# Modulation chunks in one spare place, a tenth chunk place, and split refills in a two-layer diffusion step with experts

## The chip, the cores and the metric

The kernel runs on one core of a Trainium2 chip, in one launch. The metric is device microseconds of that core, median of three runs; lower is better. The core's engines are TensorE (PE, with PEld for its weight loads), VectorE (DVE), ScalarE (ACT), GpSimd (POOL) and SyncE (SP), which here issues every DMA transfer, in program order, into one queue that 16 DMA engines share.

## The reference

Two trunk layers over 128 context tokens and 256 sample tokens, width 1024, float32. In each layer, for both token groups with the same weights:

```python
sh1, sc1, g1, sh2, sc2, g2 = silu(cond) @ w_ada + b_ada          # 6 x 1024
h = rms_norm(x, norm1_g) * (1 + sc1) + sh1
z = h @ w_in                       # four token mixers, then 4 x 1024 gate logits
branches = [conformer_conv, fourier_mix, window_attention, neighbourhood_attention]
proj = einsum("blnc,ncd->blnd", branches, w_branch)
x = x + g1 * ((sigmoid(gates) * proj).sum(n) @ w_out)
h = rms_norm(x, norm2_g) * (1 + sc2) + sh2
aff = softmax(h @ w_router)        # 16 experts, each picks its top 16 / 32 tokens
y = (silu(xs @ w_gate) * (xs @ w_up)) @ w_down * affinity
x = x + g2 * scatter_add(y)
```

At the end come one RMSNorm per group and the keys and values of the context tokens. Nearly all the traffic is weights: of 536.71 MB that the profile counts, 2 x 16 experts x 12.6 MB = 403 MB are expert weights.

## The kernel before

**Units and places.** Weights come in units of 2 MB, each one DMA transfer of 128 partitions x 4096 words: 12 modulation units a layer (ada0 to ada11), 12 of the input projection (w0 to w11), two of the branch projections (wb01, wb23) and two of the output projection (wo0, wo1). They go to a ring of seven places in SBUF (`ring`, slots 0 to 6). The list `order` is the order in which SyncE issues them, and a unit may be issued only when the unit before it in its place has been used (`used_up`). ada4, ada8 and ada9 have slot 6 (`SPARE`); ada5, ada6, ada7 and ada10 share slots 0 and 1 with the input projection, so that w4 stands behind ada5, w5 behind ada6 and w8 behind ada7. ada10 and ada11 are multiplied in the routing.

**The mixer.** TensorE, in one order written out by hand, makes 48 output tiles of the input projection (`zt`, L961; every weight is split into a high and a low part by ScalarE, L1245, and GpSimd, L893). The last 32 are the gate tiles, numbered idx 0 to 31, eight to each branch, and w4 to w11 serve four each. Between them stand attention, the branch products (L1157) and, at the numbers in `ADA_AT`, the modulation products (L701). ScalarE splits the weights of a tile two tiles ahead, in program order, so a late unit holds up all that ScalarE does after it.

**Output projection and routing.** Six tiles of products with `wo` (L1225) follow, with transposes (L1175) and router logits (L1184) between them; then a chain through VectorE and ScalarE makes the softmax and the top choice (L1685 to L1948).

**Experts.** Each expert is six chunks of 2 MB: 0 to 3 gate and up, two rows of 128 inputs (k) each, 4 and 5 down; a layer has 96, numbered x. They turn through nine places (`PLACE`): two in the arena (`LOW`, whose fourth part lies in `C` and which is thus two transfers, and `HIGH`) and the seven slots of the ring. `first_chunk` fetches 0 to 7 as their places come free, `experts_sync` the ninth and then, in order, each chunk when the chunk nine before it has been used (`used_chunk`). TensorE's products are L1800 (gate and up) and L1829 (down). Four experts make a group; a group begins with a gather of its tokens (L1768) and ends with the combination (L1846). At a layer's end SyncE issues ada0 to ada3 and w0 of the next.

Of the kernel before, what the change touches and what calls it, by code (L numbers as in the profile page):

```python
# [22 lines left out]
F32 = mybir.dt.float32  # L23
F32R = mybir.dt.float32r
ALU = mybir.AluOpType
# [115 lines left out]
def build(nc, A):  # L141
    ctx = ExitStack()
    with ctx:
# [78 lines left out]
        def adas(c):  # L222
# [36 lines left out]
        assert cursor[0] <= ARENA, cursor[0]  # L259

# [21 lines left out]
        BRL = over("BRL", "XN", 0, 8 * TOK)[:, :].rearrange("p (b c t) -> p b c t", b=4, c=2)  # L282
# [25 lines left out]
        AT = part(KT * 64).rearrange("p (k s) -> p k s", k=KT)  # L308
        assert cursor[0] <= pr_at, cursor[0]
# [10 lines left out]
                 "cum_ready sel_ready selg_ready e_pair e_down_half silu_done x_done prompt_part wo_high wo_rest mrg_high mrg_rest").split() + list(OPENING)  # L320
        land = [sem(f"land{s}") for s in range(NSLOT)]
        e_land = [sem(f"e_land{s}") for s in range(9)]
        full = [sem(f"full{b}") for b in range(8)]
        free = [sem(f"free{b}") for b in range(8)]
        e_full = [sem(f"e_full{b}") for b in range(8)]
# [3 lines left out]
            wo_high=8, wo_rest=8, mrg_high=8, mrg_rest=8, x_mixed=6, b_high=32, b_rest=32, br_high=4, br_rest=4, rest_in=16, grow_in=64, sink_in=16, cache_in=64, nab_in=16,  # L329
# [8 lines left out]
        def stood(layer, name):  # L338
# [6 lines left out]
        ADA_AT = {2: 4, 5: 5, 8: 6, 11: 7, 14: 8, 17: 9}  # L345
# [4 lines left out]
        order = ["ada0", "ada2", "ada1", "ada3", "w0", "w1", "w2", "w3", "w6", "wb01", "ada4", "w7", "ada5", "w4", "ada6",  # L350
                 "w5", "ada8", "ada7", "w8", "wb23", "ada9", "w9", "w10", "w11", "wo0", "wo1", "ada10", "ada11"]
# [5 lines left out]
        done_at.update({f"ada{c}": 23 + c for c in IN_ROUTING})  # L357
        FIXED = {"ada0": 4, "ada2": 5, "ada1": 1, "ada3": 2, "ada11": 5, "ada4": SPARE, "ada8": SPARE, "ada9": SPARE}
# [13 lines left out]
        MRGH = over("MRGH", "ring", 4 * 4 * D, KT * TOK)[:, :].rearrange("p (k t) -> p k t", k=KT)  # L372
        MRGL = over("MRGL", "arena", mrg_at, KT * TOK)[:, :].rearrange("p (k t) -> p k t", k=KT)
# [66 lines left out]
        for n in GATE_ORDER:  # L440
            for k in range(KT):
# [9 lines left out]
                if idx in ADA_AT:  # L451
                    tile_a(f"ada{ADA_AT[idx]}")
                if idx - 1 in ADA_AT:
                    ada_small_tiles(ADA_AT[idx - 1])
        for t in range(TT):
            for half in range(2):
                T.add(f"wo{t}_{half}", 2 * t + half)
# [1656 lines left out]
```

## Time and profile before

| | us |
|---|---|
| median of three runs (lowest, highest) | 1673.03 (1672.55, 1674.01) |
| the profiled execution, its own time | 1671.89 |
| its span | 1670.0 |
| TensorE products busy | 1557.3 (93%) |
| VectorE, ScalarE, GpSimd busy | 524.9, 490.0, 353.6 |
| DMA, mean over the span | 321 GB/s |

Stages overlap, and the shares are means over stages with different limits. What ends a stage is read from its own stretch: the busy share of the DMA engines there, and what TensorE waits for. In the timeline a row gives start, duration (of a merged row from the first start to the last end), engine and line, and in brackets how long the engine was idle just before, and for whom. A float32 product stands as two records.

### The profile page before, as it was taken

How to read it: one execution, taken by the hardware profiler on the slowest of the kernel's cores; microseconds unless marked ns; L12 is line 12 of the kernel's file. 1: busy time of each engine (PE TensorE's matmuls, PEld its weight loads, DVE VectorE, ACT ScalarE, POOL GpSimd, SP SyncE). 2: the span in 40 equal slices, each digit the busy share in tenths (PEclk: the TensorE clock that was granted, in tenths of full speed). 3: DMA queues.
4: the chain of work that ended last, by engine and by line, in shares of the span. 5: the costliest groups of instructions: out<-in, count | busy, mean ns of one | idle time of the engine just before them, and what ended most of it. 6: DMA issues, size and time to landing. Idle time of an engine off the chain costs nothing.

```text
span 1670.0 us, 20051 instructions
## 1 busy us (share of the span) xinstructions
PE 1557.3 (93%) x8363; PEld 956.0 (57%) x8363; DVE 524.9 (31%) x864; ACT 490.0 (29%) x908; POOL 353.6 (21%) x196
## 2 busy tenths in 40 slices
PE   7999999999999999799799999999999998988986
PEld 4998889984333343242269978899633433423322
DVE  3734454633121121121159244545411211212013
ACT  4444454433112020121153545434320211211212
POOL 1654355820000000000035634468000000000000
PEclk9999999999999999999999999999999999999999
DMA  9643452279999999999994425525799999999995
GB/s 380 243 156 110 199 202 101 105 318 425 428 426 426 426 427 427 428 427 427 422 388 168 156 102 202 202 77 232 327 423 426 426 427 428 427 427 427 427 427 233
DMA packets 52097, 536.71 MB, mean 321 GB/s; under 512 B 13584, under 2 KB 13992, under 8 KB 20008
## 3 DMA queue, kind: packets, MB, share of 16 engines
q1 hardware_dynamic: 52008, 535.43, 77.7%
q8 instruction: 67, 1.10, 0.3%
q14 instruction: 22, 0.18, 0.0%
HBM read 533.05 MB, written 2.36 MB: 321 GB/s over the span
## 4 chain that ended last, share of the span: by engine, by line
PE 68%; DMA 24%; DVE 3%; ACT 2%; issue 1%; POOL 1%; SPq 0%; DVEq 0%; ACTq 0%
PE psum L961 22%; PE psum L1800 16%; DMA ring<-in_w_e_down 14%; PE psum L1829 8%; DMA ring<-in_w_e_gu 8%; PE psum L1225 4%; PE psum L1157 3%; PE psum L1768 3%; PE psum L1846 2%; PE psum L701 2%; DMA ring<-in_w_ada 1%; DMA ring<-in_w_in 1%; PE psum L1125 1%; PE psum L695 1%; PE psum L1104 1%
## 5 line engine op out<-in xcount | busy, mean ns | idle before, releaser
L961 PE MATMUL psum<-HTH,WSR 128*128 128x384 f32 x1536 | 413.0, 341 | 8.4 <-ACT arena L1360 6.1
L1800 PE MATMUL psum<-ring,arena 128*64 128x512 f32 x1504 | 339.7, 596 | 28.1 <-DMA ring<-in_w_e_gu 26.7
L961 PEld LDWEIGHTS psum<-HTH,WSR 128*128 128x128 f32 x1536 | 280.3, 188 | 22.2 <-issue 11.6
L893 POOL TENSOR_TENSOR WSR<-ring,WSR 128x1024 fp32r<-128x1024 f32 x92 | 220.2, 2394 | 260.7 <-ACT WSR L1245 260.7
L961 PE MATMUL psum<-HTL,WSR 128*128 128x384 f32 x768 | 259.2, 337 | 0.0
L1800 PEld LDWEIGHTS psum<-ring,arena 128*64 128x64 f32 x1504 | 103.4, 137 | 233.0 <-issue 186.1
L1977 DVE TENSOR_TENSOR arena<-arena,psum 64x512 f32<-64x512 f32 x64 | 44.1, 690 | 503.6 <-PE psum L1800 315.5
L1829 PE MATMUL psum<-ring,arena 128*64 128x512 f32 x864 | 193.5, 596 | 5.2 <-DMA ring<-in_w_e_down 5.2
L1245 ACT ACTIVATE WSR<-ring 128x1024 fp32r<-128x1024 f32 x96 | 101.7, 1059 | 299.7 <-PE psum L961 289.2
L961 PEld LDWEIGHTS psum<-HTL,WSR 128*128 128x128 f32 x768 | 144.8, 189 | 0.1
L1883 ACT ACTIVATE arena<-psum 64x512 f32<-64x512 f32 x64 | 37.6, 588 | 348.5 <-PE psum L1800 348.3
L1800 PE MATMUL psum<-arena 128*64 128x512 f32 x456 | 124.0, 597 | 11.1 <-DMA C<-in_w_e_gu 7.5
L1829 PEld LDWEIGHTS psum<-ring,arena 128*64 128x64 f32 x864 | 61.1, 137 | 118.7 <-issue 117.2
L1888 ACT ACTIVATE arena<-psum 32x512 f32<-32x512 f32 x64 | 37.7, 589 | 269.7 <-PE psum L1829 269.3
L864 POOL MEMSET arena<- 128x888 f32 x2 | 2.1, 1039 | 513.0 <-PE psum L701 513.0
L1966 DVE TENSOR_TENSOR arena<-psum,GROW 32x512 f32<-32x512 f32 x64 | 43.8, 684 | 212.0 <-PE psum L1829 211.6
L624 ACT ACTIVATE arena<-psum,MOD,SC 128x128 f32<-128x128 f32 (+1 forms) x144 | 57.1, 460 | 136.1 <-PE psum L1768 130.8
L1800 PEld LDWEIGHTS psum<-arena 128*64 128x64 f32 x456 | 36.7, 136 | 82.8 <-issue 68.8
L1561 DVE TENSOR_TENSOR arena<-arena 128x384 f32<-128x384 f32 x48 | 78.6, 1638 | 1.7
L1768 PEld LDWEIGHTS psum<-arena,XN 128*128 128x128 f32 x384 | 47.0, 191 | 37.4 <-issue 37.4
L1494 DVE SCALAR_TENSOR_TENSOR psum<-arena,PRM,psum 128x414 f32<-128x414 f32 x116 | 64.7, 646 | 0.0
L1558 DVE TENSOR_TENSOR arena<-arena,psum 128x384 f32<-128x384 f32 x48 | 26.6, 554 | 113.9 <-ACT arena L1360 99.6
(221 smaller groups left out, 1730.7 us busy)
## 6 DMA issues: line engine op xcount, KB each, us to landing
ring<-in_w_e_gu SPq DMA_DIRECT2D x94, 2048.0 KB, 31.2
ring<-in_w_e_down SPq DMA_DIRECT2D x54, 2048.0 KB, 31.2
ring<-in_w_ada SPq DMA_DIRECT2D x24, 2048.0 KB, 13.1
ring<-in_w_in SPq DMA_DIRECT2D x22, 2048.0 KB, 8.0
arena<-in_w_e_gu SPq DMA_DIRECT2D x22, 1536.0 KB, 29.2
arena<-in_w_e_gu SPq DMA_DIRECT2D x12, 2048.0 KB, 29.8
arena<-in_w_e_down SPq DMA_DIRECT2D x10, 2048.0 KB, 31.5
C<-in_w_e_gu SPq DMA_DIRECT2D x22, 512.0 KB, 31.0
```

The costliest lines, as they stand in the source:

```text
L624: return nc.scalar.activation(dst, src, ACT.Identity, scale=SC[:, which, k, i:i + 1], bias=MOD[:, sec * KT + k, i:i + 1])
L893: nc.gpsimd.tensor_tensor(WSR[:, 1, i % 2], part_src(i), WSR[:, 0, i % 2].bitcast(F32), ALU.subtract).then_inc(S["w_rest"], 1)
L961: ins = nc.tensor.matmul(ps[:, 0:TOK], WSR[:, w, i % 2, k, :], x[:, k, :], start=(k == 0 and w == 0 and x is HTH), stop=(k == KT - 1 and w ...
L1157: ins = nc.tensor.matmul(ps[:, 0:TOK], w[:, idx % 2, c, :], x[:, c, :], start=(ins is None), stop=(c == 1 and w is BWL))
L1225: ins = nc.tensor.matmul(ps[:, :], x[:, k, t * P:(t + 1) * P], w[half][:, k, :], start=(k == 0 and turn == 0), stop=(k == KT - 1 and turn ...
L1245: nc.scalar.activation(WSR[:, 0, i % 2], part_src(i), ACT.Copy).then_inc(S["w_high"], 1)
L1494: ins = nc.vector.scalar_tensor_tensor(acc if k < CONV_K - 1 else ACC[:, c, :], U[:, c, k:k + AW], w, acc, ALU.mult, ALU.add)
L1561: nc.vector.tensor_tensor(MRG[:, k, :], MRG[:, k, :], GP[:, idx % 2, :], ALU.add).then_inc(S["gate_add"], 1)
L1768: ins = nc.tensor.matmul(ps[:, c0:c0 + P], XN[:, t, k * P:(k + 1) * P], SEL[:, AT_PLACE[t]].rearrange("p e s -> p (e s)"), start=(t != 2), ...
L1800: ins = nc.tensor.matmul(pb[half][64 * m:64 * m + 64, :], XE[:, k, j, :], w[:, half * CH:(half + 1) * CH], start=(k == 0), stop=(k == KT - 1))
L1829: ins = nc.tensor.matmul(ps[64 * half:64 * half + 64, :], AT[:, k, :], chunk_row(x, k % 4)[:, half * CH:(half + 1) * CH], start=(k == 0), ...
L1977: e_release(nc.vector.tensor_tensor(AA[0:64, cols], TMP[64:128, cols], ps[64:128, :], ALU.mult), f"gu{j}_{half}")
```

## The change

- ada4 to ada10 all go through the spare place (slot 6), one after the other. The order of the units is new: w4, w5 and w8 go ahead of ada5, ada6 and ada7, ada8 after ada7, ada10 before w10. ada10 is multiplied in the mixer, at idx 20.
- The merged branches' high part (`MRGH`) moves from slot 4 to `XN`, the low part of the last branch to slot 5, half of the squares to the arena and the transposed activations (`AT`) into `XE`. So slot 4 is free once the last attention output is copied, and takes chunk 0, which is issued after w11. Slot 0 takes chunk 1, after wo1.
- Chunk 8 goes once to a tenth place, half in `GROW[:, 0]` and half in `once_slot`, after the residual sum and the router's exponentials. It is never refilled; the others turn through nine places as before.
- Chunks 10, 11 and 12 come as two transfers each (the last of them, in `LOW`, as three instead of two), the first half when the first half of the place is used (`e_first`), the rest at the old wait. The last gate-up chunk comes as halves, the last down chunk as quarters, and the last expert takes both halves of the output row after row.
- Router: three idle products instead of one, after the last logits; the last transpose goes ahead of the logits of its tile. The combination waits for halves of the last expert's output, and the last output row goes out in two halves.

```diff
@@ units
-        ADA_AT = {2: 4, 5: 5, 8: 6, 11: 7, 14: 8, 17: 9}
+        ADA_AT = {2: 4, 5: 5, 8: 6, 11: 7, 14: 8, 17: 9, 20: 10}
...
-                 "w5", "ada8", "ada7", "w8", "wb23", "ada9", "w9", "w10", "w11", "wo0", "wo1", "ada10", "ada11"]
+                 "ada6", "w8", "ada7", "ada8", "wb23", "ada9", "w9", "ada10", "w10", "w11", "wo0", "wo1", "ada11"]
...
-        FIXED = {"ada0": 4, "ada2": 5, "ada1": 1, "ada3": 2, "ada11": 5, "ada4": SPARE, "ada8": SPARE, "ada9": SPARE}
+        FIXED = {"ada0": 4, "ada2": 5, "ada1": 1, "ada3": 2, "ada11": 5, **{f"ada{c}": SPARE for c in range(4, 11)}}
@@ places of the chunks
-            PLACE = (LOW, HIGH, unit_at["wo0"][0], SPARE, unit_at["wo1"][0], 3, 4, unit_at["ada10"][0], unit_at["ada11"][0])
+            third = 3 - unit_at["wo0"][0] - unit_at["wo1"][0]
+            PLACE = (4, third, LOW, HIGH, unit_at["wo0"][0], SPARE, unit_at["wo1"][0], 3, unit_at["ada11"][0])
...
+            ONCE = RING - 1
+
+            LAST_UP, LAST_DOWN = NE * PER - 3, NE * PER - 1
...
+                if x == ONCE:
+                    sp.dma_start(GROW[:, 0].rearrange("p i d -> p (i d)"), src[:, 0:2 * D]).then_inc(once_land, 16)
+                    sp.dma_start(once_slot, src[:, 2 * D:4 * D]).then_inc(once_land, 16)
+                    return
+                if x == LAST_DOWN:
+                    for r in range(4):
+                        sp.dma_start(chunk_row(x, r), src[:, r * D:(r + 1) * D]).then_inc(down_land[r], 16)
+                    return
...
@@ first_chunk, and when
+                    if s == 4:
+                        copied(sp, f"o{len(ATT) - 1}")
...
+                    elif name == "w11":
+                        first_chunk(0)
                     elif name == "wo1":
-                        first_chunk(0)
-                sp.wait_ge(S["out_kv"], base("out_kv") + 64)
-                for x in range(1, RING - 1):
+                        first_chunk(1)
+                        sp.wait_ge(S["out_kv"], base("out_kv") + 64)
+                        first_chunk(2)
+                for x in range(3, RING - 1):
                     first_chunk(x)
@@ experts_sync
+                sp.wait_ge(S["x_mixed"], base("x_mixed") + 2 * TT)
+                sp.wait_ge(S["router_exp"], base("router_exp") + 1)
+                fetch(sp, ONCE, chunk(l, ONCE // PER, ONCE % PER))
                 used_up(sp, "ada11")
...
-                for x in range(RING, NE * PER):
-                    used_place_of(x - RING)
-                    fetch(sp, x, chunk(l, x // PER, x % PER))
+                for x in range(RING + 1, NE * PER):
+                    before_it = turn(x) - RING + (turn(x) - RING >= ONCE)
+                    src = chunk(l, x // PER, x % PER)
+                    if before_it < PAIRS - 1:
+                        sp.wait_ge(S["e_first"], base("e_first") + before_it + 1)
+                        fetch_first_rows(sp, x, src)
+                        used_place_of(before_it)
+                        fetch_last_rows(sp, x, src)
+                    else:
+                        used_place_of(before_it)
+                        fetch(sp, x, src)
...
@@ router, TensorE
+                transposed(2, 1)
                 logits(2, 0)
-                transposed(2, 1)
-                idle_products(T.at["wo2_0"][0], 1)
                 logits(2, 1)
-                ada_main(pe, l, 10)
+                idle_products(T.at["wo2_1"][0], 3)
@@ experts_tensor, gate and up
+                            if g == 0 and j == 0 and k in (0, 2, 4):
+                                ins.then_inc(S["e_first"], 1)
```

On SyncE in the mixer of a layer, the seven transfers after the context keys and values have gone out, before: ada5, w4, ada6, w5, ada8, ada7, w8.

```order
L848 DMA ring<-in_w_ada 128x4096 [waits w_rest]
L848 DMA ring<-in_w_in 128x4096 [waits full0]
L848 DMA ring<-in_w_ada 128x4096 [waits w_rest]
L848 DMA ring<-in_w_in 128x4096 [waits full2]
L848 DMA ring<-in_w_ada 128x4096 [waits full2]
L848 DMA ring<-in_w_ada 128x4096 [waits w_rest]
L848 DMA ring<-in_w_in 128x4096 [waits full3]
```

The same seven in the list of after: w4, ada5, w5, ada6, w8, ada7, ada8.

```order
L908 DMA ring<-in_w_in 128x4096 [waits w_rest]
L908 DMA ring<-in_w_ada 128x4096 [waits full2]
L908 DMA ring<-in_w_in 128x4096 [waits w_rest]
L908 DMA ring<-in_w_ada 128x4096 [waits full0]
L908 DMA ring<-in_w_in 128x4096 [waits w_rest]
L908 DMA ring<-in_w_ada 128x4096 [waits full2]
L908 DMA ring<-in_w_ada 128x4096 [waits full3]
```

Each weight unit moved ahead of the modulation unit that had shared its place. w4 now waits for a tile of w6 alone (`w_rest`), and each ada for the products with the one before it (`full`).

On SyncE at the end of the mixer, before: wo0 and wo1, chunk 0 (arena and C), ada10, ada11, chunk 1, then chunks 2 to 8 and the first of the two transfers of chunk 9, a refill.

```order
L848 DMA ring<-in_w_out 128x4096 [waits w_rest] x2
L568 DMA arena<-in_w_e_gu 128x3072 [waits full2]
L569 DMA C<-in_w_e_gu 128x1024
L848 DMA ring<-in_w_ada 128x4096 [waits b_rest]
L848 DMA ring<-in_w_ada 128x4096 [waits full3]
L571 DMA arena<-in_w_e_gu 128x4096 [waits gate_add,out_kv]
L571 DMA ring<-in_w_e_gu 128x4096 [waits full4] x2
L571 DMA ring<-in_w_e_down 128x4096 [waits full5] x2
L571 DMA ring<-in_w_e_gu 128x4096 [waits full5]
L571 DMA ring<-in_w_e_gu 128x4096 [waits full0]
L571 DMA ring<-in_w_e_gu 128x4096 [waits full1]
L568 DMA arena<-in_w_e_gu 128x3072 [waits e_pair]
```

After, from chunk 0 on: it stands ahead of wo0 and wo1; then chunks 1 and 2, ada11, chunks 3 to 7, chunk 8 in two, and chunk 9, the last before the refills.

```order
L604 DMA ring<-in_w_e_gu 128x4096 [waits free2]
L908 DMA ring<-in_w_out 128x4096 [waits w_rest] x2
L604 DMA ring<-in_w_e_gu 128x4096 [waits b_rest]
L601 DMA arena<-in_w_e_gu 128x3072 [waits full2,out_kv]
L602 DMA C<-in_w_e_gu 128x1024
L908 DMA ring<-in_w_ada 128x4096 [waits full3]
L604 DMA arena<-in_w_e_gu 128x4096 [waits gate_add]
L604 DMA ring<-in_w_e_down 128x4096 [waits full2] x2
L604 DMA ring<-in_w_e_gu 128x4096 [waits full1] x2
L587 DMA GROW<-in_w_e_gu 128x2048 [waits router_exp,x_mixed]
L588 DMA arena<-in_w_e_gu 128x2048
L604 DMA ring<-in_w_e_gu 128x4096 [waits full1]
```

Chunk 0 went ahead of the output projection's units, ada10 is gone from here, and ten chunks instead of nine stand ahead of the first refill, the ninth of them as halves that wait for the router's exponentials.

## Rows read from the trace of the kernel before

**Rows 1.** page: the span, and the DMA engines' busy tenths in 40 slices

```profile
span 1670.0 us, 20051 instructions
...
DMA  9643452279999999999994425525799999999995
```

**Rows 2.** chain of waits, layer 1's expert stage: start us, us, what

```profile
1208.19 1.94 PE psum L1800 x8
...
1299.44 7.02 PE psum L1829 x32
...
1315.20 1.94 PE psum L1800 x8
...
1609.61 40.32 DMA ring<-in_w_e_down
1650.06 3.65 PE psum L1829 x16
```

**Rows 3.** busy time by stretch: five engines, granted clock, DMA share, GB/s

```profile
364.20:372.70 8.50, 8.50 (x53) 7.38 (x51) 2.97 (x6) 3.12 (x6) 0.00 (x0) 1.00 0.02 10
372.70:827.90 455.20, 415.41 (x2008) 160.31 (x2009) 81.63 (x147) 76.18 (x158) 0.00 (x0) 1.00 1.01 425
```

**Rows 4.** timeline of SyncE's issues, layer 0: first refills

```profile
372.11 0.80 SPq L571 DMA_DIRECT2D ring<-in_w_e_down  x2
...
405.11 0.33 SPq L571 DMA_DIRECT2D ring<-in_w_e_down  x1
...
409.17 0.33 SPq L571 DMA_DIRECT2D ring<-in_w_e_gu  x1
...
414.91 0.33 SPq L571 DMA_DIRECT2D ring<-in_w_e_gu  x1
```

**Rows 5.** timeline of TensorE, layer 0, first expert, k = 4

```profile
399.73 1.94 PE L1800 MATMUL psum<-ring,arena 128*64 128x512 f32 x8
```

**Rows 6.** timeline, both mixers: issues of ada5 and w4, and who waits

```profile
129.44 0.35 SPq L848 DMA_DIRECT2D ring<-in_w_ada  x1
...
160.11 0.35 SPq L848 DMA_DIRECT2D ring<-in_w_in  x1
...
168.18 1.06 ACT L1245 ACTIVATE WSR<-ring 128x1024 fp32r<-128x1024 f32 x1 [4.87 <-DMA ring<-in_w_in]
...
171.09 0.57 PE L961 MATMUL psum<-HTH,WSR 128*128 128x384 f32 x1 [3.26 <-ACT arena L1360]
...
992.04 0.45 PE L961 MATMUL psum<-HTH,WSR 128*128 128x384 f32 x1 [2.82 <-ACT arena L1360]
```

**Rows 7.** busy time by stretch, behind the two waits of TensorE

```profile
171.00:174.50 3.50, 3.41 (x11) 3.41 (x12) 2.21 (x4) 0.72 (x3) 1.36 (x2) 0.54 0.16 66
...
992.00:995.50 3.50, 3.46 (x19) 3.46 (x20) 2.22 (x4) 0.67 (x2) 1.32 (x2) 1.00 0.27 115
```

**Rows 8.** timeline, layer 0: issue of ada7, and TensorE's products with it

```profile
196.48 0.33 SPq L848 DMA_DIRECT2D ring<-in_w_ada  x1
...
208.61 1.92 PE L701 MATMUL psum<-ring,condT 128*32 128x512 f32 x16
```

**Rows 9.** timeline, layer 0's router: ada10's products, VectorE's affinities

```profile
376.99 1.92 PE L701 MATMUL psum<-ring,condT 128*32 128x512 f32 x16
...
378.67 0.21 DVE L1694 TENSOR_TENSOR arena<-arena 128x48 f32<-128x48 f32 x1
```

**Rows 10.** timeline of ScalarE, opening of layer 1: w0

```profile
852.95 1.06 ACT L1245 ACTIVATE WSR<-ring 128x1024 fp32r<-128x1024 f32 x1 [1.14 <-DMA ring<-in_w_in]
```

**Rows 11.** timeline of TensorE, last expert: last gate-up chunk, first down half

```profile
1640.23 3.65 PE L1800 MATMUL psum<-ring,arena 128*64 128x512 f32 x16 [1.24 <-DMA ring<-in_w_e_gu]
...
1645.98 3.65 PE L1829 MATMUL psum<-ring,arena 128*64 128x512 f32 x16
```

**Rows 12.** DMA issues: queue, operation, count, KB each, us to landing

```profile
C<-in_w_e_gu SPq DMA_DIRECT2D x22, 512.0 KB, 31.0
...
out_y_sample<-XN SPq DMA_DIRECT2D x2, 512.0 KB, 2.7
```

More of the change, by code:

```diff
@@ L1165, in mixer_tensor @@
                             ada_main(pe, l, ADA_AT[idx])
-                        if idx - 1 in ADA_AT:
+                        if idx - 1 in ADA_AT and ADA_AT[idx - 1] not in IN_ROUTING:
                             ada_small(ADA_AT[idx - 1])
@@ L1377, in mixer_scalar @@
                         ins.then_inc(S["exps_done"], 1)
-                    if idx in ADA_AT:
+                    if idx in ADA_AT and ADA_AT[idx] not in IN_ROUTING:
                         copy_out(f"ada{ADA_AT[idx]}", adas(ADA_AT[idx]), lambda ps: ps)
@@ L1617, in mixer_vector @@
                                                 ALU.mult).then_inc(S["p_ready"], 1)
[L1618 removed]
+                    if idx - 1 in ADA_AT and ADA_AT[idx - 1] not in IN_ROUTING:
                         ada_end(ADA_AT[idx - 1])
@@ L1727, in experts_sync @@
                     for name in ("ada0", "ada2", "ada1", "ada3", "w0"):
-                        used_place_of(max(x for x in range(NE * PER) if PLACE[x % RING] == unit_at[name][0]))
+                        used_place_of(max(x for x in range(NE * PER) if x != ONCE and PLACE[turn(x) % RING] == unit_at[name][0]))
                         if name == "w0":
@@ L1736, in experts_sync @@
                         dst = A["y_prompt"] if t == 0 else A["y_sample"][:, (t - 1) * P:t * P]
-                        sp.wait_ge(once["fin_y"], i + 1)
-                        sp.dma_start(dst.rearrange("b s d -> (b s) d"), XN[:, t, :]).then_inc(once["fin_out"], 16)
-                    sp.wait_ge(once["fin_out"], TT * 16)
+                        rows = dst.rearrange("b s d -> (b s) d")
+                        if i < TT - 1:
+                            sp.wait_ge(once["fin_y"], i + 1)
+                            sp.dma_start(rows, XN[:, t, :]).then_inc(once["fin_out"], 16)
+                        else:
+                            for half in range(2):
+                                cols = slice(half * CH, (half + 1) * CH)
+                                sp.wait_ge(once["fin_y"], TT + half)
+                                sp.dma_start(rows[:, cols], XN[:, t, cols]).then_inc(once["fin_out"], 16)
+                    sp.wait_ge(once["fin_out"], (TT + 1) * 16)
             def experts_tensor(pe):
@@ L1786, in gate_up @@
                         pb = [e_open(pe, g, f"gu{j}_{half}") for half in range(2)]
-                        for k, halves in [(k, (0, 1)) for k in range(KT - 2)] + [(k, (half,)) for half in range(2) for k in (KT - 2, KT - 1)]:
+                        last_two = [(k, (half,)) for half in range(2) for k in (KT - 2, KT - 1)]
+                        if g * GRP + j == NE - 1:
+                            last_two = [(KT - 2, (0, 1)), (KT - 1, (0, 1))]
+                        for k, halves in [(k, (0, 1)) for k in range(KT - 2)] + last_two:
                             if j == 0 and 0 in halves and 0 < k < KT - 1:
```

146 lines of the change are left out of this document (100 added, 46 removed).

## The prediction

> **What bounds the kernel now.** I read the page's slices first, then the chain of waits of the second layer, then busy time by stretch around the router, then the DMA issues of SyncE, and last the waits of TensorE in the mixers. The slices [rows 1] show two kinds of stage: in the expert stages (slices 10 to 21 and 30 to 39) the DMA engines are at 9, in the mixers mostly at 2 to 6, with a slice of 7 ahead of each expert stage that hides a hole. The chain [rows 2] ends in 40.32 us of waiting for expert weights and then the last 16 products: the expert stage ends when its last chunk lands. How long TensorE alone would need follows from the same rows: a group of four experts that waits for no DMA takes 1315.20 - 1208.19 = 107.0 us from group to group and 1299.44 + 7.02 - 1208.19 = 98.3 us to its last down product, so four need 3 x 107.0 + 98.3 = 419.3 us. They took 1650.06 + 3.65 - 1208.19 = 445.5. So weights that come up to 26 us sooner still set the end.
>
> The stretches [rows 3] show the hole: for 8.5 us, while the output projection ends, the DMA engines do nothing (share 0.02); then they run at 1.01 for 455.2 us, in which 92 of the 96 chunks pass, 4.95 us each. The second layer has the same pair of stretches. So a chunk fetched ahead of the hole takes 4.95 us off its layer, as long as no new hole opens behind it.
>
> **The change part by part.**
>
> *Two chunks more ahead of the hole.* Before, chunks 0 to 3 precede it, with two modulation units in the same queue. After, chunk 0 goes out after w11, when the last attention output is copied, in a time of slices at 2 [rows 1], and unit ada10 leaves the stretch for the mixer, so six chunks precede the hole. 2 x 4.95 = 9.9 us a layer. The hole itself stays: chunks 6 and 7 still wait for the last output product, as the issue at 372.11 does [rows 4].
>
> *The new hole behind it.* After, chunk x would start at 372.7 + 4.95(x - 6), and chunks 10 to 14 may only be issued when chunks 0 to 4 are used. The same frees stand in the trace of before: chunk 2 at 405.11, chunk 3 at 409.17, chunk 4 at 414.91 [rows 4], and an issue has to come 0.6 us ahead of its transfer (372.11 to the 372.7 at which the engines wake, rows 3 and 4). Chunk 12 is due at 402.4, so issued whole it would be 405.11 - 401.8 = 3.3 late; halved, its first half goes when the k = 4 products end (399.73 + 1.94 = 401.7, [rows 5]), in time, and its second is due at 404.3 and 0.8 late. Chunk 13: due at 407.4, 409.17 - 406.8 = 2.4 late. Chunk 14: due at 412.3, 414.91 - 411.7 = 3.2 late. Later chunks are freed at the pace of the products, 98.3 / 24 = 4.1 us each, and due every 4.95, so the largest of these is the whole hole: 3.2 us. The halving alone is worth 0.1, for chunk 14 is whole and as late. Bounds: 0, if the products start earlier, and 9.9, if frees slip until nothing is gained. I take 3.2, since the rows name the same waits. Stream: -9.9 + 3.2 = -6.7 us a layer, -13.4 in two. The tenth place is in this: without it each of these frees would be due 4.95 earlier.
>
> *The spare place.* In before, w4 is issued only when ada5 has been multiplied (160.11), since they share a place; ScalarE waits for it until 168.18, TensorE stands still for 3.26 us and, in layer 1, for 2.82 [rows 6]. In layer 0 the granted clock then is 0.54 over 3.5 us [rows 7], which costs 3.5 x 0.46 = 1.6; in layer 1, after the shorter wait, it is 1.00. After, w4 takes the issue that ada5 had, 129.44 [rows 6], and lands long before. -4.9 and -2.8 us, on the path, as TensorE is busy on both sides. Bound: a stall of the same length could show at the next late unit, w5; but w5 too goes out one use of a modulation unit sooner than before, so I take the whole.
>
> *What that place makes late.* ada7 is now queued right behind w8. Both used to be issued apart: ada7 at 196.48 for products at 208.61 [rows 8], 12.1 us. One transfer takes 168.18 - 160.11 = 8.1 us to be usable [rows 6]; behind another it takes 8.1 + 4.95 = 13.0. TensorE waits 0.9 us in each layer; queued behind ada7 on SyncE are ada8 and wb23, which wait for later products anyway. Bounds 0 and 5. The other modulation units follow no long transfer that is issued with them as late as this, and I cost them at nothing.
>
> *ada10 in the mixer.* Its products are 1.92 us. In the router they ended at 378.91, with VectorE at 378.88 the later condition of what follows [rows 9], so taking them away there gives 0, and the three idle products stand in the same wait (bounds -0.8 and +0.4). In the mixer, where TensorE has no gap, they cost 1.92 a layer.
>
> *Opening of layer 1.* ScalarE waits 1.14 us for w0, the end of the DMA queue [rows 10], so it moves with the stream and the shorter tail of layer 0 gives nothing more. 0, bounds -1.1 and +0.5.
>
> *The tail of layer 1.* The last gate-up chunk in halves lets TensorE use the 1.24 us that it waited at 1640.23 [rows 11]. The first down half then starts not at 1645.98 but when chunk 94 lands, 1650.06 - 4.95 = 1645.1, and ends at 1648.8. Three quarters of the last chunk cost 3/4 x 3.65 = 2.7 and have landed: 1651.5; the last quarter 0.9: 1652.4 instead of 1653.7. -1.3. The last output transfer is half as long, 0.26 MB less at 425 GB/s: -0.6. Together -1.9, bounds 0 and -2.5. The half waits at the combination give nothing, since idle products stand ahead of it.
>
> New places for the rest of the branches, the squares and the transposed activations change no count of instructions on a full engine: 0, bounds +-0.5.
>
> **Sum.** Layer 0: -4.9 + 0.9 + 1.9 - 6.7 = -8.8. Layer 1: -2.8 + 0.9 + 1.9 - 6.7 - 1.9 = -8.6. Together -17.4 on the profiled execution's 1671.89 (span 1670.0 [rows 1]): 1654.5. The median, 1673.03, is 1.1 above that execution: **1655.6 us**.
>
> **The rivals.** (1) *The hole only moves* (0.08): frees slip, the 9.9 us are given back in each layer. For it: three of the refills are late already. Against it: the lateness would have to be three times the worst row. The rest, -17.4 + 13.4 = -4.0, gives 1669.
>
> (2) *The spare place becomes a chain* (0.12): each modulation unit waits for the one before, SyncE waits with it, and TensorE stalls at ada7 by the 5 us of the bound, with the clock of rows 7 after it (1.6). For it: SyncE is one queue, and seven units now pass one place. Against it: only ada7 stands directly behind a transfer that is issued late. 2 x (5 + 1.6 - 0.9) = 11.4: 1667.
>
> (3) *Each extra transfer costs a gap* (0.04), the slower side: the change issues 8 transfers more per layer (one for chunk 8, three for the halves, one for the last gate-up chunk, three for the last down chunk) and one at the end, 17. An output transfer of 0.52 MB takes 2.7 us to land [rows 12], 1.2 of which are its bytes at 425 GB/s; if the other 1.5 were paid in the queue, 17 x 1.5 = 25.5: 1681. It decides from 17.4 / 17 = 1.0 us a transfer on. Against it: 22 chunks of before already go as two transfers [rows 12], inside stretches at 1.01 [rows 3]. By the Trainium skill (DMA: Bandwidth & Descriptors, section Anatomy of one DMA) a DMA pays about 2.0 us beside its bytes, most of it the receipt of the last write; 17 of them would by that be 34 us, and by that page the change would lose. The trace does not agree for a queue that is never empty: the share of 1.01 has no room for it.
>
> (4) *No new hole* (0.12): router and first expert run some us sooner, ada7 comes in time. -2 x (3.2 + 0.9) - 1.1: 1646.
>
> **How the numbers follow.** The forecast has 0.61, with its own range of 1650 to 1661 (the hole at 1 to 5 us a layer, the stalls and the tail at half or full). A change without effect on the stream and with the mixer's two costs unpaid, within 0.2% (3.3 us, which is what a measurement of this kernel can tell from none), has 0.03. The range of 1647 to 1665 leaves out rivals 1 to 3 for the most part and the best of rival 4. Faster by over 0.2%: the forecast, 2, 4 and three quarters of 1, which lies at that bound: 0.91. Within it: the 0.03 and the rest of 1, 0.05. Slower: rival 3, 0.04.
>
> **What would show it.** The dead stretch ahead of the first refills should still be there, about 8 us, with six chunks in front of it and a second, short one of about 3 us some 35 to 45 us later; each expert stage at a share of 1.0 behind it for about 6.7 us less in all. The stalls at ScalarE's wait for w4 should be gone and the clock full there; a wait of about 1 us for ada7 should stand at its products. The last products should end about 2.4 us after the last bytes, not 3.7. Wrong it would be if the share in the expert stage fell below 1.0 throughout (rival 3), or if the second dead stretch were 8 us or longer (rival 1).

## The result, and the profile after

The changed kernel takes **1655.39 us** in the median (1653.87 to 1661.22, 4 runs), the kernel before 1673.05 beside it; the ratio is 0.9897, 95% interval [0.9875, 0.992]. The forecast was 1655.6. The profiled execution took 1656.3, its span is 1654.5, so 15.5 us less than in [rows 1].

Page of the changed kernel: span, and the DMA engines' slices.

```profile
span 1654.5 us, 20149 instructions
...
DMA  9733454379999999999994443535799999999996
```

I cut the span at events that both traces have (first mixer product, last output product, last down product) and set the difference beside the forecast:

| stretch | before | after | difference | forecast |
|---|---|---|---|---|
| start to mixer 0 | 36.22 | 36.97 | +0.75 | 0 |
| mixer 0, to the last output product | 335.87 | 334.81 | -1.06 | -2.1 |
| router and experts 0 | 461.13 | 455.15 | -5.98 | -8.0 (stream -6.7, tail -1.3) |
| opening of layer 1 | 24.86 | 24.64 | -0.22 | +1.3 (the tail waits for w0) |
| mixer 1 | 333.41 | 334.01 | +0.60 | 0.0 |
| router and experts 1 | 462.22 | 453.44 | -8.78 | -8.0 |
| last down product to the end | 16.29 | 15.48 | -0.81 | -0.6 |
| sum | 1670.0 | 1654.5 | -15.5 | -17.4 |

The first row is no effect of the change: it is 35.7 to 37.4 us in the runs below, whose openings are alike.

Busy time by stretch of the changed kernel, to hold against [rows 3] (last three columns: granted clock, DMA share, GB/s): the dead stretch of each layer, then what follows it.

```profile
363.00:372.40 9.40, 9.40 (x57) 8.10 (x56) 2.98 (x6) 3.60 (x7) 0.00 (x0) 1.00 0.07 31
372.40:390.00 17.60, 16.33 (x78) 9.94 (x77) 11.71 (x37) 5.77 (x13) 0.00 (x0) 0.81 0.99 400
390.00:425.00 35.00, 33.65 (x173) 13.83 (x173) 4.63 (x8) 10.27 (x22) 0.00 (x0) 1.00 0.96 362
425.00:440.00 15.00, 13.97 (x72) 5.15 (x70) 1.80 (x3) 1.56 (x3) 0.00 (x0) 1.00 1.01 429
...
1178.30:1186.40 8.10, 8.10 (x52) 7.11 (x50) 2.65 (x7) 3.12 (x6) 0.00 (x0) 1.00 0.01 4
1186.40:1260.00 73.60, 69.62 (x357) 29.99 (x358) 19.34 (x48) 18.77 (x39) 0.00 (x0) 1.00 1.00 407
```

The dead stretch is still there, about 8 us (the first row has 0.7 us of earlier transfers in it), with six chunks ahead of it. The new hole is no dead stretch but a thin stream, and the share hides it; the bytes show it. At 427 GB/s, what the queue runs at later, the three stretches of layer 0 lack (17.6 x 27 + 35 x 65 - 15 x 2) / 427 = 6.4 us, layer 1's lacks 73.6 x 20 / 427 = 3.4. The same count on before:

```profile
372.70:440.00 67.30, 63.06 (x337) 27.41 (x338) 18.14 (x47) 17.70 (x37) 0.00 (x0) 1.00 1.00 419
1192.00:1260.00 68.00, 63.76 (x340) 27.66 (x341) 18.25 (x47) 17.71 (x37) 0.00 (x0) 1.00 1.00 417
```

gives 1.3 and 1.6, so the new hole is 5.1 us in layer 0 and 1.8 in layer 1; 3.2 were forecast for each. Why they differ stands in the router, layer 0 first, then layer 1 (same columns):

```profile
374.00:376.00 2.00, 1.92 (x14) 1.86 (x14) 1.12 (x4) 0.96 (x2) 0.00 (x0) 0.78 0.84 360
376.00:378.00 2.00, 2.00 (x5) 1.39 (x6) 1.02 (x5) 1.44 (x4) 0.00 (x0) 0.50 0.99 426
378.00:380.00 2.00, 2.00 (x4) 0.82 (x4) 0.75 (x3) 0.02 (x1) 0.00 (x0) 0.50 0.98 418
...
1188.00:1190.00 2.00, 1.93 (x15) 1.72 (x16) 1.16 (x5) 1.16 (x2) 0.00 (x0) 1.00 0.89 377
1190.00:1192.00 2.00, 2.00 (x12) 0.87 (x14) 1.41 (x7) 1.26 (x4) 0.00 (x0) 1.00 1.07 459
```

In layer 0 the granted clock falls to 0.50 (1.2 GHz); from the last output product to the first expert product it takes 390.47 - 371.78 = 18.7 us there and 15.8 in layer 1, where before took 16.7 in both. TensorE's rows ahead of the fall:

```profile
371.38 0.40 PE L1288 MATMUL psum<-WOL,MRGH 128*128 128x512 f32 x1
371.61 1.85 PE L1247 MATMUL psum<-arena 128*128 128x16 f32 x16
373.31 0.64 PE L1238 MATMUL psum<-C,X 128*128 128x128 f32 x4
373.79 2.63 PE L1247 MATMUL psum<-arena 128*128 128x16 f32 x16
376.25 4.19 PE L753 MATMUL psum<-C 128*128 128x384 f32 x6
...
390.47 1.94 PE L1884 MATMUL psum<-ring,arena 128*64 128x512 f32 x8 [0.32 <-ACT arena L682]
```

16 logits products of 16 columns (32 records; the expectations below, and the prediction in its "last 16 products", count records) follow one another, with four transposes; the idle products, moved behind them, begin when the clock is already down. The same ends of the router in layer 1, and in layer 0 of before:

```profile
1185.18 0.40 PE L1288 MATMUL psum<-WOL,MRGH 128*128 128x512 f32 x1
...
1201.40 1.94 PE L1884 MATMUL psum<-ring,arena 128*64 128x512 f32 x8 [0.32 <-ACT arena L682]
```

```profile
371.69 0.40 PE L1225 MATMUL psum<-WOL,MRGH 128*128 128x512 f32 x1
...
388.80 1.94 PE L1800 MATMUL psum<-arena 128*64 128x512 f32 x8 [0.32 <-ACT arena L624]
```

SyncE's issues in layer 0's mixer and the refills behind the router, for [rows 4, 6, 8]; then TensorE's products with ada7; then busy time around w4's first use, for [rows 7], in both layers:

```profile
130.71 0.35 SPq L908 DMA_DIRECT2D ring<-in_w_in  x1
...
192.81 0.33 SPq L908 DMA_DIRECT2D ring<-in_w_in  x1
193.19 14.84 SPq L908 DMA_DIRECT2D ring<-in_w_ada  x2
...
410.85 0.33 SPq L604 DMA_DIRECT2D arena<-in_w_e_gu  x1
416.59 0.33 SPq L604 DMA_DIRECT2D ring<-in_w_e_gu  x1
```

```profile
205.73 1.92 PE L759 MATMUL psum<-ring,condT 128*32 128x512 f32 x16 [0.86 <-DMA ring<-in_w_ada]
...
1019.53 1.92 PE L759 MATMUL psum<-ring,condT 128*32 128x512 f32 x16 [0.72 <-DMA ring<-in_w_ada]
```

```profile
130.00:200.00 70.00, 69.80 (x461) 59.56 (x460) 30.60 (x53) 34.05 (x69) 31.39 (x21) 1.00 0.40 155
945.00:1015.00 70.00, 69.80 (x462) 59.56 (x461) 30.58 (x53) 34.05 (x69) 30.39 (x20) 1.00 0.43 161
```

w4 goes out at 130.71, and the waits and the low clock of [rows 6, 7] are gone: TensorE stands still for 0.2 of 70 us, at the full clock. ada7 goes out behind w8, and its products wait 0.86 and 0.72 us. Chunk 14 (416.59) is the latest refill: 416.59 + 0.6 - (372.4 + 8 x 4.95) = 5.2 us.

The last expert, for [rows 11], and the last DMA bytes (columns as above):

```profile
1631.93 3.65 PE L1917 MATMUL psum<-arena 128*64 128x512 f32 x16 [0.76 <-DMA arena<-in_w_e_down]
1635.39 3.63 PE L1917 MATMUL psum<-ring,arena 128*64 128x512 f32 x16
```

```profile
1635.00:1636.00 1.00, 1.00 (x8) 0.48 (x6) 0.00 (x0) 0.00 (x0) 0.00 (x0) 1.00 0.34 139
1636.00:1637.00 1.00, 1.00 (x7) 0.34 (x4) 0.00 (x0) 0.00 (x0) 0.00 (x0) 1.00 0.03 12
```

The products end at 1639.0. These rows count a packet where it starts; the last packet of the chunk ends at 1636.4 by the trace, 2.7 us before the products do. In before it ends at 1649.5, 4.2 us before them (1653.7).

### The profile page after: what moved, and what is told of

The parts are those of the page before. It is cut to its first block, busy times and chain, and to the rows that moved or that the text cites. A ratio compares the mean times of both kernels' runs of the same rounds, so it can differ in the third digit from the quotient of the medians.

```text
span 1654.5 us, 20149 instructions
## 1 busy us (share of the span) xinstructions
PE 1559.8 (94%) x8371; PEld 962.9 (58%) x8371; DVE 525.4 (32%) x865; ACT 489.7 (30%) x908; POOL 353.3 (21%) x196
## 4 chain that ended last, share of the span: by engine, by line
PE 76%; DMA 16%; DVE 3%; ACT 2%; POOL 1%; issue 1%; SPq 1%; DVEq 0%; ACTq 0%
PE psum L1024 22%; PE psum L1884 21%; PE psum L1917 11%; DMA ring<-in_w_e_down 5%; DMA arena<-in_w_e_down 5%; PE psum L1288 4%; PE psum L1220 3%; DMA ring<-in_w_ada 3%; PE psum L1847 3%; DMA ring<-in_w_e_gu 2%; PE psum L1934 2%; PE psum L759 2%; DMA ring<-in_w_in 1%; PE psum L753 1%; DVE arena L2078 1%
## 5 line engine op out<-in xcount | busy, mean ns | idle before, releaser
L1884 PE MATMUL psum<-ring,arena 128*64 128x512 f32 x1472 | 331.6, 596 | 20.3 <-DMA ring<-in_w_e_gu 18.4
L1024 PEld LDWEIGHTS psum<-HTH,WSR 128*128 128x128 f32 x1536 | 280.7, 188 | 16.7 <-issue 12.8
L1917 PE MATMUL psum<-ring,arena 128*64 128x512 f32 x864 | 193.3, 595 | 2.9 <-DMA ring<-in_w_e_down 2.9
L1884 PE MATMUL psum<-arena 128*64 128x512 f32 x472 | 127.5, 596 | 7.6 <-DMA arena<-in_w_e_gu 4.3
L1847 PEld LDWEIGHTS psum<-arena,XN 128*128 128x128 f32 x384 | 46.9, 191 | 37.4 <-issue 37.4
```

What stands on the lines that cost most here:

```text
L1024: ins = nc.tensor.matmul(ps[:, 0:TOK], WSR[:, w, i % 2, k, :], x[:, k, :], start=(k == 0 and w == 0 and x is HTH), stop=(k == KT - 1 and w ...
L1847: ins = nc.tensor.matmul(ps[:, c0:c0 + P], XN[:, t, k * P:(k + 1) * P], SEL[:, AT_PLACE[t]].rearrange("p e s -> p (e s)"), start=(t != 2), ...
L1884: ins = nc.tensor.matmul(pb[half][64 * m:64 * m + 64, :], XE[:, k, j, :], w[:, half * CH:(half + 1) * CH], start=(k == 0), stop=(k == KT - 1))
L1917: ins = nc.tensor.matmul(ps[64 * half:64 * half + 64, :], XE[:, k, j, :], chunk_row(x, k % 4)[:, half * CH:(half + 1) * CH], start=(k == 0 ...
```

## The experiments

Ratios are to the kernel before, run on the same chip with each group (its median 1673.2 to 1675.5). One per mille is 1.7 us. The profile of each run gives its stretches, cut as in the table.

**The order of the units alone**, in the kernel before.

```diff
-        order = [... "w7", "ada5", "w4", "ada6", "w5", "ada8", "ada7", "w8", "wb23", ...]
+        order = [... "w7", "w4", "ada5", "w5", "ada6", "w8", "ada7", "ada8", "wb23", ...]
-        FIXED = {... "ada4": SPARE, "ada8": SPARE, "ada9": SPARE}
+        FIXED = {... **{f"ada{c}": SPARE for c in range(4, 10)}}
```

> The kernel before, with the spare place for the modulation units and the new order of the units alone (w4 ahead of ada5, w5 ahead of ada6, w8 ahead of ada7); ada10 stays in the routing, nine places, whole refills, whole tail. Theory: TensorE's waits for w4 (3.26 and 2.82 us) and the 1.6 us at the low clock go, two waits of 0.9 us at ada7's products come: -4.9 + 0.9 - 2.8 + 0.9 = -5.9, 1667.1 against 1673.0, with the expert stages as long as before. Rival (the spare place is a chain): ada7's products wait 5 us and the clock falls behind them, -4.9 - 2.8 + 2 x 6.6 = +5.5: 1678.5. Second rival: the expert stage ends with the DMA queue whatever the mixer does, so nothing is gained: 1673.

0.9953 [0.9941, 0.9965], -7.9 us; 1668.06. In its profile the mixers take 331.64 and 331.84, so -4.2 and -1.6 (forecast -4.0 and -1.9), and from the first expert product to the last down product it is as long as before (444.8 and 445.6; before, 444.4 and 445.5). The waits at ada7:

```profile
203.91 1.92 PE L701 MATMUL psum<-ring,condT 128*32 128x512 f32 x16 [0.91 <-DMA ring<-in_w_ada]
...
1022.09 1.92 PE L701 MATMUL psum<-ring,condT 128*32 128x512 f32 x16 [1.43 <-DMA ring<-in_w_ada]
```

The mixer term is shown by itself; the chain of 5 us falls, and so does the rival that the mixer gains nothing. Against this run the mixers of the changed order (eight runs, 333.5 to 335.9) are 2.5 us longer in the mean of either layer: ada10, forecast at 1.9, and whatever else the change moved there. Its products take the 1.92; the rest was not taken apart.

**Nine places.**

```diff
-            ONCE = RING - 1
+            ONCE = -1
...
-                return x if x < ONCE else x - 1
+                return x
...
-                fetch(sp, ONCE, chunk(l, ONCE // PER, ONCE % PER))
                 used_up(sp, "ada11")
-                fetch(sp, RING, chunk(l, RING // PER, RING % PER))
+                fetch(sp, RING - 1, chunk(l, (RING - 1) // PER, (RING - 1) % PER))
...
```

> The changed kernel without the tenth place: chunk 8 goes to the place that ada11 leaves, and every later chunk waits for the one nine before it (the halved refills are chunks 9, 10 and 11); the split of the last gate-up chunk is in two transfers. Theory: the same frees are due one chunk, 4.95 us, sooner, so the hole behind the first refills grows by 4.95 us in each layer: +9.9 on the changed kernel, 1665.3. Rival (the hole is not set by the places, but by the start of the first expert, or the later slack makes up for it): less than 3 us, 1655 to 1658.

0.9936 [0.9923, 0.9949], 6.5 us above the changed kernel, with intervals too wide to tell 3 from 9.9; the stretches decide. From the last output product to the last down product it takes 458.4 us in layer 0 and 462.0 in layer 1. Layers whose routers ran at the same clock take 452.3 and 456.1 in the changed kernel (below), so +6.1 and +5.9; 1.5 of layer 0's are a low clock at its last down products, which the opening of layer 1 hides, so 4.6 and 5.9 are the place's. The tenth place is worth what was forecast, about 5 us a layer; the rival of less than 3 falls. Against before (461.1 and 462.2) this run's stretches are only 2.7 and 0.2 us shorter (the second with its router at the low clock, 2.2 us longer), though six chunks precede the hole in it too and that alone was to save 9.9: without the place, most of it comes back as a longer hole.

**Whole refills.**

```diff
-            HALVED = range(RING + 1, RING + PAIRS)
+            HALVED = range(0)
...
```

> The changed kernel with its first three refills (chunks 10, 11, 12) issued whole again. Theory (the last late refill sets the hole, and chunk 14, whole in both, is as late as any): from the changed kernel's trace chunk 14 comes 416.59 + 0.6 - 412.0 = 5.2 us late in layer 0, and a whole chunk 12 would be 406.78 + 0.6 - 402.1 = 5.3 late, so 0.1 us a layer: the time stays within 1 us of the changed kernel's 1655.4, and DMA moves as many bytes in the 70 us behind the first refills. Rival (each refill that is issued late loses its own time): the three first halves go 2.7, 2.7 and 3.4 us sooner than whole chunks would, so 2.7 to 8.8 us a layer are lost without them: 1661 to 1673.

0.9899 [0.9882, 0.9915], no difference. Both its routers ran at the full clock; the stretches are 453.7 and 455.0, +1.4 and +1.5, the second with its last down products at the low clock (1.4). The halves are worth 0.1 to 1.4 us a layer, more than the 0.1 forecast in one layer, and nothing like the 2.7 to 8.8 of the rival.

**Every chunk in two transfers, cut along its rows**: the 16 KB of each partition as two of 8 KB, 186 transfers more (likewise for the places in two parts).

```diff
-                    sp.dma_start(high_slot if s == HIGH else ring[:, s, :], src).then_inc(landing, 16)
+                    sp.dma_start(dst[:, 0:2 * D], src[:, 0:2 * D]).then_inc(landing, 16)
+                    sp.dma_start(dst[:, 2 * D:4 * D], src[:, 2 * D:4 * D]).then_inc(landing, 16)
...
```

> The changed kernel with every expert chunk in one transfer more (two instead of one, or three instead of two), 96 - 3 = 93 a layer besides the last halves, 186 more in all. Theory: in a queue that is never empty a transfer costs nothing beside its bytes: the share stays 1.0 and the time within 3 us of 1655.4. Rival (each transfer pays a gap; 1.0 us was the point at which the change would have lost): 186 x 1.0 = +186 us, 1841; at 0.1 us still +19, 1674.

0.9949 [0.9933, 0.9966], 8.7 us above the changed kernel: 0.05 us a transfer (0.02 to 0.07 by the two intervals). This run's row, then the changed kernel's:

```profile
460.00:760.00 300.00, 277.48 (x1323) 107.63 (x1321) 52.18 (x82) 48.71 (x103) 0.00 (x0) 1.00 1.01 420
```

```profile
460.00:760.00 300.00, 281.85 (x1345) 109.35 (x1343) 52.19 (x82) 48.72 (x103) 0.00 (x0) 1.00 1.01 427
```

The theory of no price and the rival of 1.0 us are both wrong, the rival by twenty times: by this the change's 17 transfers cost an estimated 0.8 us. The share is the same in both rows; only GB/s tells.

**Every chunk in two transfers, cut between partitions.**

```diff
-                    sp.dma_start(high_slot if s == HIGH else ring[:, s, :], src).then_inc(landing, 16)
+                    for ps in (slice(0, 64), slice(64, P)):
+                        sp.dma_start(dst[ps, :], src[ps, :]).then_inc(landing, 16)
...
```

> The changed kernel with every expert chunk in one transfer more, as in the run with two transfers each, but cut between partitions 0 to 63 and 64 to 127, so that the rows stay 16 KB long and the packets as many as in the changed kernel (54.5 thousand, not 81). That run lost some 9 us and its queue ran at 420 GB/s where the others have 427. Theory a (the price is one of transfers, 9 / 186 = 0.05 us each): the same here, 420 GB/s and about 1664. Theory b (the price is one of packets, 9 us for 27 thousand more on 16 engines): 427 GB/s here and 1655 to 1657. Rival: a transfer on half the partitions uses fewer of the DMA engines at a time, and the stream falls far below 420 GB/s.

1.428 [1.42, 1.436]; the profiled execution took 2380.35 us.

```profile
460.00:760.00 300.00, 194.89 (x629) 65.20 (x629) 22.22 (x35) 20.44 (x42) 0.00 (x0) 0.77 1.01 223
```

The rival's outcome holds, half the rate; its reason does not, for at a mean share of 1.01 the engines are not idle: a packet of 16 KB took 1.18 us here, in the mean of this stretch, and 0.62 in the changed kernel. So the run can't tell whether transfers or packets cost the 0.05 us. The packets of the run before it say more: one of 8 KB took 314 ns there, half of one of 16 KB in the changed kernel is 308. That is the lost 2% of the rate, inside the packets; no gap between transfers shows in the share.

**ada7 first.**

```diff
-                 "ada6", "w8", "ada7", "ada8", ...
+                 "ada6", "ada7", "w8", "ada8", ...
```

> The changed kernel with unit ada7 issued ahead of w8 instead of behind it. Theory (TensorE waits 0.86 and 0.72 us at ada7's products because w8's bytes precede it in the queue): both waits go, w8 has some 30 us to its first use and stays hidden, the mixers are 0.8 us shorter each, and since what comes sooner out of the mixer comes sooner out of the expert stage, the whole is 1.6 us shorter: about 1653.8 where the changed kernel has 1655.4. Rival: ada7 is late because it waits for its place, not for w8: the waits stay, 1655.4. Second rival: w8 comes late in its turn and TensorE waits for it up to 4.95 us: 1660 or more.

0.991 [0.9891, 0.9928]: no gain in time. In the profile no product with ada7 waits any more and the mixers, 333.9 and 333.4, are hardly shorter than the changed order's 333.5 to 335.9; but both its routers ran at a low clock (17.4 and 18.9 us), and both its last experts. The wait's cause is shown, its worth in time is not.

**An idle product between the transposes and the last logits.**

```diff
                 transposed(2, 1)
+                idle_products(T.at["wo2_1"][0], 1)
                 logits(2, 0)
                 logits(2, 1)
-                idle_products(T.at["wo2_1"][0], 3)
+                idle_products(T.at["wo2_1"][0], 2)
```

> The changed kernel with one of the three idle products moved between the last transposes and the last router logits. Theory: the granted clock falls to 0.5 in some of the routers (layer 0 of the changed kernel, layer 1 of the run with nine places) because 32 products of 16 columns follow one another there, where the kernel before has an idle product of 384 columns among them; with one between them the clock stays at 1.0 in both layers, from the last output product to the first expert product it takes 15.8 + 0.8 = 16.6 us in both, not 15.8 or 18.8, and the expert stage has no layer with the late start. On the time -2 us where a router would have been slow, +0.8 where not: 1654 to 1657. Rival (the fall has nothing to do with the order of these products): one of the two layers takes 18 us or more all the same.

0.9892 [0.9878, 0.9907], no difference in time; both routers take 16.2 us.

**The kernel before without its idle product in the router.**

```diff
-                idle_products(T.at["wo2_0"][0], 1)
```

> The kernel before without the idle product that stands between the last transposes and the last router logits. Theory (this product is what keeps the granted clock up through the router): the clock falls to 0.5 in at least one of the two routers, and that one takes 18 us or more from the last output product to the first expert product, against 16.7 in both layers of before; the other stays at 16.7. Rival (the fall in the changed kernel comes from its longer run of logits, or from something else): both stay at 16.7 and the time at that of before, 1673 to 1675.

1.0007 [0.9997, 1.0016]; both routers take 19.3 and 19.5 us, not 16.7.

```profile
377.00:379.00 2.00, 1.44 (x8) 1.47 (x8) 0.86 (x4) 1.22 (x2) 0.00 (x0) 0.70 1.01 434
379.00:381.00 2.00, 2.00 (x14) 0.65 (x17) 1.19 (x6) 0.71 (x3) 0.00 (x0) 0.50 1.04 442
```

With the two runs the cause is shown: where an idle product stands among the logits the clock holds (10 of 10 routers: before, the order alone, and the three versions with it), without it in the changed order it falls in 8 of 16, and without it in before in 2 of 2. In before TensorE also stands still there, for the transposes' copy (1.44 of 2.00 us busy), in the changed order it does not; so this run does not tell the stop from the narrow products. The time is that of before, for less of the delay is paid here: with routers 2.6 and 2.8 us longer, it takes 2.4 and 0.8 longer from the last output product to the last down product.

**The changed kernel again.**

> The changed kernel once more, unaltered, for its two routers and for a comparison on the same chip with the version below. Theory (whether the clock falls in a router of this order is open from execution to execution): of its two routers, from the last output product to the first expert product, one takes 15.8 us and one 17 to 19, or both the same; where it takes longer, the expert stage of that layer ends later by as much. Time 1655 to 1658. Rival (the fall belongs to layer 0 of this kernel): layer 0 some 18.7, layer 1 15.8 as in the first profile.

1656.22, 0.9897 [0.988, 0.9913]. Here the clock fell in layer 1 (18.7) and not in layer 0 (15.8), so it doesn't belong to a layer. The same stretches of the same kernel now give the price: 452.3 against 455.15 in layer 0 and 456.1 against 453.44 in layer 1. The 2.9 us that the router is late come out at the end of the layer as 2.9 and 2.7.

**The tail whole**, with the order of its products and its waits for chunks as in before; the half waits at the combination stay.

```diff
-                if x == LAST_DOWN:
+                if False:
                     for r in range(4):
...
-                if x == LAST_UP:
+                if False:
...
-                        for cols in ((slice(0, D),) if i < TT - 1 else (slice(0, CH), slice(CH, D))):
+                        for cols in (slice(0, D),):
```

> The changed kernel without the parts of the tail: last gate-up and last down chunk and last output in one transfer each, and the order of the last products as before. Theory: only layer 1 pays, 1.3 us at the last down products (its last products end 3.7 us after the last chunk has landed, not some 2.4) and 0.6 us at the last output: +1.9, 1657.3; in layer 0 the products end 1.3 us later too, but the opening of layer 1 waits for w0 in the queue and starts as before. Rival: both layers pay, +3.2: 1658.6. Second rival: nothing, since the DMA queue ends both: 1655.4.

0.9917 [0.9893, 0.994], 3.3 us above the changed kernel, too wide to tell 1.9 from 3.2. By its profile the last products end 4.2 us after the end of the last packet (1637.1 to 1641.3), as in before, against 2.7: 1.5 us for the quarters. From there to the end it takes 15.51, with the split output 15.48: the half output is worth nothing.

**A joined version**: the edits of *ada7 first* and of the idle product, and chunk 14 in halves.

```diff
-            HALVED = range(RING + 1, RING + PAIRS)
+            HALVED = (*range(RING + 1, RING + PAIRS), RING + PAIRS + 1)
...
+                            if g == 0 and j == 0 and k == 1:
+                                ins.then_inc(S["e_first"], 1)
```

> A version meant to beat both: the changed kernel with ada7 ahead of w8, one idle product between the last transposes and the last logits, and the refill of chunk 4's place (chunk 14) in halves too, its first half sent after the first two down rows of the first expert. Theory: ada7's waits go (-0.7 us a layer), both routers take 16.2 us (-1.3 us a layer on the mean of 15.8 and 18.8), and chunk 14, the latest refill at 2.7 us in the run with the idle product, comes 1.8 us sooner, which leaves chunk 13 as the latest at 1.9: -0.8 us a layer. Together about -5 us: 1650 to 1652 where the changed kernel has 1655.4. Rival (the gains in the mixer are taken back by the opening of layer 1 or by other late refills): 1654 to 1656.

0.9878 [0.9863, 0.9892], 1654.09: 2.1 us better than the changed kernel beside it (the intervals overlap), not 5. Both routers took 16.2. Chunk 14 in halves shows no gain where 0.8 us a layer was expected: from the first expert product to the last down product, less the low clock shown below, it takes 437.2 and 437.7 us, with the idle product alone 436.3 and 437.5. Another part of the miss is in the tail:

```profile
1629.12 5.35 PE L1918 MATMUL psum<-arena 128*64 128x512 f32 x16 [0.81 <-DMA arena<-in_w_e_down]
1634.27 3.63 PE L1918 MATMUL psum<-ring,arena 128*64 128x512 f32 x16
```

The first down products of the last expert ran at the low clock, 1.7 us longer. Over the runs up to here (but the one at half the rate) that is so in 8 of 16 last experts with the last down chunk in quarters and in none of 8 with it whole.

**The joined version with idle products in the last expert's two waits.**

```diff
+                                if g * GRP + j == NE - 1 and k == 0:
+                                    idle_products(E.at[f"gu{j - 1}_0"][0], 1)
                                 e_copied(pe, g, f"gu{j}_{k // 4}")
...
+                        if g * GRP + j == NE - 1:
+                            idle_products(E.at[f"gu{j - 1}_0"][0], 1)
                         ps = e_open(pe, g, f"y{j}")
```

> The joined version (ada7 first, idle product in the router, chunk 14 in halves) with two more idle products in the last expert of each layer: one in the 0.70 us in which TensorE waits for VectorE ahead of the first transposes, one in the 0.8 us in which it waits for the first quarter of the last down chunk. In the profiles so far the granted clock falls to 0.5 behind these waits in about half of the last experts whose down chunk comes in quarters (the first down products take 5.0 to 5.4 us there, not 3.65), in none where it comes whole. Theory: with the waits filled the first down products take 3.65 us in both layers; in layer 1 that is 1.7 us at the end, in layer 0 w0 hides it: 1652.4 against 1654.1, ratio to before 0.9867. Rival (the idle products only come on top, or the clock falls all the same): 1654 to 1655.

0.9867 [0.9851, 0.9883], 1651.09 us (1650.42 to 1654.83): the best of all, 0.3% below the changed kernel, though the intervals overlap a little. In both layers the first down products take 3.65 us, but two of two are too few to show the cause where it is so in 8 of 16 without. The second wait is for the down chunk ahead of the last, which comes whole. Layer 1's last expert:

```profile
1629.59 0.91 PE L753 MATMUL psum<-C 128*128 128x384 f32 x2
1630.45 3.65 PE L1922 MATMUL psum<-arena 128*64 128x512 f32 x16
1633.92 3.62 PE L1922 MATMUL psum<-ring,arena 128*64 128x512 f32 x16
```

## Why the prediction was right, step by step

**Right, with its size:** the stalls at w4 (-4.2 and -1.6 by the order alone, net of the wait at ada7; forecast -4.0 and -1.9); the wait at ada7 (0.86 and 0.72, in the other runs of this order 0.4 to 2.0; forecast 0.9); the tenth place (4.6 and 5.9 a layer; 4.95); the tail in quarters (-1.5 by the end of the last packet; -1.3), though it is given back where the clock falls behind its waits; the dead stretch, which stayed. The rule used for the hole, that the latest refill sets it and not the sum, is borne out by the run with whole refills.

**Right in sum, wrong in the part:** the hole. 3.2 us were forecast for each layer from the frees of before, with the router at 0 and bounds of -0.8 and +0.4. The router term failed, outside both bounds: it is -0.9 us at the full clock and +2.0 at the low one. At the full clock the logits end 4.1 us after the last output product, in before 5.0: the idle product no longer stands ahead of the last of them. I took the three idle products to stand in a wait, and so they do, but did not ask what the one that they replace had done for the clock. Since the frees follow the router, the hole is 1.8 or 5.1, and the mean, 3.4, happens to lie at the forecast. That is luck: the profiled execution had one router of each kind, and with two alike the same kernel would by the 2.9 and 2.7 us above have come out nearly 3 us to either side, an estimate.

**Mis-sized:** what the change adds to the mixer, 2.5 us for ada10's 1.9. The end: -0.8 for -0.6, but not by the half output, which gives 0: the half waits at the combination, put at nothing, let it start 1.33 us after the last down product, not 1.69, and spare the row statistics a wait of 0.3. The halves of the refills: 0.1 to 1.4 for 0.1.

**The opening:** ScalarE's wait for w0 grew as forecast, from 1.14 [rows 10] to 2.41:

```profile
847.46 1.06 ACT L1307 ACTIVATE WSR<-ring 128x1024 fp32r<-128x1024 f32 x1 [2.41 <-DMA ring<-in_w_in]
```

Yet the opening isn't 1.3 us longer, but 0.2 shorter: w0's wait had been read as the one that ends last, and it wasn't. ScalarE's next copy, before and after:

```profile
854.90 0.60 ACT L1239 ACTIVATE arena<-psum 128x512 f32<-128x512 f32 x1 [0.90 <-PE psum L701]
```

```profile
848.42 0.58 ACT L1301 ACTIVATE arena<-psum 128x512 f32<-128x512 f32 x1
```

In before ScalarE stood idle 0.90 us more behind w0, for TensorE's products with a modulation unit, so of the 1.3 us only 0.4 reach the path. The combination, which starts 0.4 us sooner here as it does at the end, makes up for that and 0.2 more.

**The rivals:** the chain and the loss by transfers fall, each by a run of its own; the hole that only moves falls by the expert stretches, 6.0 and 8.8 us shorter. *No new hole* came near in the layers at the full clock. Against the price of transfers I had argued that a share of 1.01 has no room for it. That argument was wrong, though its conclusion held: the share is 1.01 at 420 GB/s and at 223 too. The 2.0 us a DMA that the Trainium skill states (DMA: Bandwidth & Descriptors, Anatomy of one DMA) stand there for DMAs that GpSimd issues, and most of them are the wait until the last write is confirmed; in SyncE's queue, never empty, the run with 186 transfers more shows 0.05.

## What to carry to other kernels

When places come free too late behind a hole, the latest free sets the end, and every microsecond by which the first consumer starts later can be paid in full at the end of the stage, even where TensorE has 26 us to spare (2.9 and 2.7 of 2.9 us in the changed kernel, 2.4 and 0.8 of 2.6 and 2.8 in before). A fetch ahead of the hole pays only with a place behind it. Ask of an idle or filler product that is moved what it kept up where it stood: the granted clock is such a thing, and a fall that comes in half of the routers hides in a median. Read GB/s beside the DMA share.

## What the runs showed of the hardware

- A transfer on 64 partitions moved at half the rate: 223 GB/s against 427, at a share of 1.01 in both. The Trainium skill (Advanced Engine Details and Errata, DMA Bandwidth Details) ties each of the 16 ports into the memory to 8 partitions, so 64 partitions would reach 8 of them; the measured rate fits that.
- 186 more transfers along the rows cost 8.7 us, 0.05 each, and lower the stream from 427 to 420 GB/s; packets of 8 KB took 314 ns, of 16 KB 616.
- The clock can fall without TensorE being idle: in the router of layer 0, in 16 products of 16 columns and four transposes, it was busy for 1.92 to 2.00 of every 2 us, as the profile counts, while the clock went from 1.00 to 0.50. In 8 of 16 routers with that order it fell.
